# Block attention by pairs of heads in the second block of a two-block transformer kernel

## What is computed

```python
s_own = jnp.einsum('bhqd,bhkd->bhqk', q_c, k_own).astype(f32) + bias_own.astype(f32)[None]
s_own = jnp.where(own_pos[None, :] <= q_pos[:, None], s_own, -jnp.inf)
...
probs = jax.nn.softmax(logits, axis=-1).astype(v.dtype)
...
out = ... + jnp.einsum('bhqk,bhkd->bhqd', p_own, v_own)
```

## Time and profile before

| | us |
|---|---|
| median of 3 runs | 2380.49 (2379.0 to 2385.83) |
| the profiled execution | 2381.41 |
| its span in the profile | 2379.6 |
| TensorE busy in the span | 2307.9 (97%) |
| VectorE busy | 1080.0 (45%) |
| ScalarE busy | 432.1 (18%) |
| mean granted TensorE clock | 0.987 of full speed |

### The profile page before, as it was taken

The page is one execution under the profiler, slowest core; times in us unless marked ns, Lnnn a source line. Parts: engine busy times, 40 slices in busy tenths (PEclk is TensorE's granted clock), DMA queues, the critical chain, the costliest instruction groups (busy, mean ns, idle before and its releaser), DMA issues. The chain is left out here.

```text
span 2379.6 us, 28978 instructions
## 1 busy us (share of the span) xinstructions
PE 2307.9 (97%) x12084; PEld 1560.1 (66%) x12084; DVE 1080.0 (45%) x2030; ACT 432.1 (18%) x850; POOL 47.1 (2%) x76
## 2 busy tenths in 40 slices
PE   6999999999999989999999999999999999999998
PEld 4778854444444468658767768748857867676873
DVE  2788331111111166652453356666663155235674
ACT  1122221111111121100322211101101122221110
POOL 1000000000000010000000000000000000000000
PEclk9999999999999989999999999999999999999999
DMA  9656569999999954444230444436544242134541
GB/s 397 242 225 270 197 202 371 422 422 422 422 422 422 401 164 158 165 162 151 76 135 20 159 151 158 161 124 212 177 159 176 93 156 90 43 136 150 177 168 44
DMA packets 175981, 499.74 MB, mean 210 GB/s; under 512 B 6888, under 2 KB 99320, under 8 KB 146048
## 3 DMA queue, kind: packets, MB, share of 16 engines
q1 hardware_dynamic: 171904, 481.23, 53.7%
q0 software_dynamic: 3824, 16.43, 2.2%
q10 hardware_dynamic: 144, 0.52, 0.1%
HBM read 491.34 MB, written 6.82 MB: 209 GB/s over the span
## 5 line engine op out<-in xcount | busy, mean ns | idle before, releaser
L2104 PE MATMUL bank<-Tw,Sx 128*128 128x256 f32 x960 | 213.8, 379 | 0.0
L2104 PEld LDWEIGHTS bank<-Tw,Sx 128*128 128x128 f32 x960 | 179.3, 190 | 22.7
L2192 PE MATMUL bank<-xT,ring 128*128 128x256 f32 x704 | 152.6, 379 | 0.0
L862 PE MATMUL bank<-xT,ring 128*128 128x256 f32 x640 | 143.4, 384 | 2.8 <-ACT xT L279 2.8
L2192 PEld LDWEIGHTS bank<-xT,ring 128*128 128x128 f32 x704 | 133.4, 190 | 18.0
L2104 PE MATMUL bank<-ring,xT 128*128 128x256 f32 x640 | 144.7, 379 | 0.0
L862 PEld LDWEIGHTS bank<-xT,ring 128*128 128x128 f32 x640 | 122.6, 193 | 21.8 <-ACT xT L279 2.9
L2104 PEld LDWEIGHTS bank<-ring,xT 128*128 128x128 f32 x640 | 121.6, 190 | 18.2 <-issue 1.9
L1425 PE MATMUL bank<-ring,xg 128*64 128x512 f32 x512 | 113.9, 593 | 5.3 <-DMA ring<-in_w 5.3
L1462 PE MATMUL bank<-ring,hTg 128*64 128x512 f32 x512 | 113.4, 595 | 0.0
L1425 PE MATMUL bank<-more,xg 128*64 128x512 f32 x512 | 112.6, 592 | 0.0
(11 more groups left out here) (515 smaller groups left out, 3602.6 us busy)
## 6 DMA issues: line engine op xcount, KB each, us to landing
ring<-in_w SPq DMA_DIRECT2D x128, 1024.0 KB, 17.5
ring<-in_ffn_w_in SPq DMA_DIRECT2D x88, 1024.0 KB, 7.7
ring<-in_first_pieces SPq DMA_DIRECT2D x33, 2048.0 KB, 12.1
more<-in_w SPq DMA_DIRECT2D x64, 1024.0 KB, 17.3
ring<-in_ffn_w_out SPq DMA_DIRECT2D x20, 2048.0 KB, 7.9
ring<-in_w_mix_in SPq DMA_DIRECT2D x12, 2048.0 KB, 7.7
ring<-in_xattn_w_kv SPq DMA_DIRECT2D x8, 2048.0 KB, 8.0
ring<-in_w_mix_out SPq DMA_DIRECT2D x4, 2048.0 KB, 9.8
```

Of the source, the lines that this page charges most:

```text
L862: last = nc.tensor.matmul(b[:, c * SEQ:(c + 1) * SEQ], w[:, k, m * P:(m + 1) * P], xT[:, k, :], start=(k == 0), stop=(k == KD - 1))
L2104: last = nc.tensor.matmul(bank[BANK_OF[name]][:, 0:SEQ], lhs(k), rhs(k), start=(k == 0), stop=(k == 3))
L2192: last = nc.tensor.matmul(b[:, c * SEQ:(c + 1) * SEQ], w[:, k, col:col + P], xT[:, k, :], start=(k == 0), stop=(k == KD - 1))
```

## The change

The loop over eight heads becomes one over four pairs on all three engines. TensorE now issues the scores of both heads product by product in turns (low rows, high rows), the transposes of both heads in a row, and the values of both heads in turns (low columns, high columns). A filler is cut in two parts per pair, one ahead of the values and one behind. `mats(l, 1)` and `mats(l, 3)` stand with one row half at the end of the pairs 0 and 1 and with the other behind the scores in the pairs 1 and 2. ScalarE does the two copies of a pair, then the two exponentials of the next pair; the exponential of head 1 comes ahead of `take_kv(3)`. VectorE does the two `probs` of a pair, then the two `logits` of the next, then the `diagonal` and `inverse_start` calls. No tile, bank or DMA is added, and the count of products is the same.

```diff
--- before.py
+++ after.py
@@ -2309,36 +2309,45 @@
                             last.then_inc(mat_full, 1)
 
             def moba_attention(l):
-                def scores(h):
-                    r = slice((h % 2) * 64, (h % 2) * 64 + 64)
-                    if h >= 2:
-                        pe.wait_ge(mb_sb, l * NH + (h - 1))
-                    b = bank[4 + h % 2]
-                    nc.tensor.matmul(b[:, 0:P], qm[r, h // 2, 0:P], km[r, h // 2, 0:P], start=True, stop=True)
-                    nc.tensor.matmul(b[:, P:384], qm[r, h // 2, P:SEQ], km[r, h // 2, :],
-                                     start=True, stop=True).then_inc(at_s, 1)
-
-                def turned(h):
-                    pe.wait_ge(at_p, l * N_AT + (h + 1))
-                    if h >= 2:
-                        pe.wait_ge(at_tc, l * N_AT + (h - 1))
-                    b = bank[6 + h % 2]
-                    for c, (dst, src) in enumerate(((0, 0), (P, P), (2 * P, 2 * P))):
-                        last = nc.tensor.transpose(b[:, dst:dst + P], sm[:, h % 2, src:src + P], eye)
-                    last.then_inc(at_t, 1)
-
-                def values(h):
-                    pe.wait_ge(at_tc, l * N_AT + (h + 1))
-                    r = slice((h % 2) * 64, (h % 2) * 64 + 64)
-                    o = bank[2 + h // 4][r, ((h // 2) % 2) * SEQ:((h // 2) % 2 + 1) * SEQ]
-                    hs = slice(h * 64, (h + 1) * 64)
-                    nc.tensor.matmul(o, vm[:, 0, hs], pmT[:, h % 2, 0:SEQ], start=True, stop=False)
-                    nc.tensor.matmul(o[:, P:SEQ], vm[:, 1, hs], pmT[:, h % 2, SEQ:384],
-                                     start=False, stop=True).then_inc(at_o, 1)
+
+
+                def half(h):
+                    return slice((h % 2) * HD, (h % 2) * HD + HD)
+
+                def scores(p):
+                    if p:
+                        pe.wait_ge(mb_sb, l * NH + 2 * p)
+                    heads = (2 * p, 2 * p + 1)
+                    for h in heads:
+                        nc.tensor.matmul(bank[4 + h % 2][:, 0:P], qm[half(h), p, 0:P], km[half(h), p, 0:P],
+                                         start=True, stop=True)
+                    for h in heads:
+                        nc.tensor.matmul(bank[4 + h % 2][:, P:384], qm[half(h), p, P:SEQ], km[half(h), p, :],
+                                         start=True, stop=True).then_inc(at_s, 1)
+
+                def turned(p):
+                    pe.wait_ge(at_p, l * N_AT + (2 * p + 2))
+                    if p:
+                        pe.wait_ge(at_tc, l * N_AT + 2 * p)
+                    for h in (2 * p, 2 * p + 1):
+                        for c in range(3):
+                            last = nc.tensor.transpose(bank[6 + h % 2][:, c * P:(c + 1) * P],
+                                                       sm[:, h % 2, c * P:(c + 1) * P], eye)
+                        last.then_inc(at_t, 1)
+
+                def values(p):
+                    pe.wait_ge(at_tc, l * N_AT + (2 * p + 2))
+                    heads = (2 * p, 2 * p + 1)
+                    o = bank[2 + p // 2][:, (p % 2) * SEQ:(p % 2 + 1) * SEQ]
+                    for h in heads:
+                        nc.tensor.matmul(o[half(h), :], vm[:, 0, h * HD:(h + 1) * HD], pmT[:, h % 2, 0:SEQ],
+                                         start=True, stop=False)
+                    for h in heads:
+                        nc.tensor.matmul(o[half(h), P:SEQ], vm[:, 1, h * HD:(h + 1) * HD], pmT[:, h % 2, SEQ:384],
+                                         start=False, stop=True).then_inc(at_o, 1)
 
                 pe.wait_ge(lora_act, (l + 1) * N_LORA)
                 scores(0)
-                scores(1)
                 cross_kv(l, 1)
                 bonus(l)
                 cross_kv(l, 2)
@@ -2347,26 +2356,27 @@
                 mats(l, 2)
                 cross_kv(l, 3)
 
-                low, high = range(0, 4), range(4, KD)
+                quarters = [range(n, n + 2) for n in range(0, KD, 2)]
                 if l == 0:
-                    fill = {0: [(6, low)], 1: [(6, range(4, 6))], 2: [(6, range(6, KD))], 3: [(7, range(0, 2))],
-                            4: [(7, range(2, 4))], 5: [(7, range(4, 6))], 6: [(7, range(6, KD))]}
+                    fill = [((6 + p // 2, quarters[2 * (p % 2)]), (6 + p // 2, quarters[2 * (p % 2) + 1]))
+                            for p in range(NH // 2)]
                 else:
-                    fill = {0: [(4, low), (4, high)], 1: [(5, low)], 2: [(5, high)], 3: [(6, low)], 4: [(6, high)],
-                            5: [(7, low)], 6: [(7, high)]}
-                for h in range(NH):
-                    if h == 0:
+                    fill = [((4 + p, range(0, 4)), (4 + p, range(4, KD))) for p in range(NH // 2)]
+                for p in range(NH // 2):
+                    if p == 0:
                         pe.wait_ge(mat_dve, l * N_MDVE + 4)
-                    turned(h)
-                    if h + 2 < NH:
-                        scores(h + 2)
-                    if h == 4:
+                    turned(p)
+                    if p < NH // 2 - 1:
+                        scores(p + 1)
+                    if 0 < p < 3:
+                        mats(l, 2 * p - 1, (1,))
+                    cross_kv(l, *fill[p][0])
+                    if p == 2:
                         pe.wait_ge(mat_dve, l * N_MDVE + 8)
-                    values(h)
-                    for g, ks in fill.get(h, ()):
-                        cross_kv(l, g, ks)
-                    if h < 4:
-                        mats(l, 1 + 2 * (h // 2), (h % 2,))
+                    values(p)
+                    cross_kv(l, *fill[p][1])
+                    if p < 2:
+                        mats(l, 2 * p + 1, (0,))
 
             def rwkv_heads(l):
 
@@ -2727,20 +2737,25 @@
                 for g in range(3):
                     take_kv(g)
                 expo(0)
+                expo(1)
                 take_kv(3)
-                for h in range(NH):
-                    if h + 1 < NH:
-                        expo(h + 1)
-                    act.wait_ge(at_t, l * N_AT + (h + 1))
-                    if h >= 2:
-                        act.wait_ge(at_o, l * N_AT + (h - 1))
-                    nc.scalar.activation(pmT[:, h % 2, :], bank[6 + h % 2][:, 0:384], ACT.Copy).then_inc(at_tc, 1)
-                    if h % 2 and (l or h > 3):
-                        take_kv(4 + h // 2)
-                    if h % 4 == 3:
-                        act.wait_ge(at_o, l * N_AT + (h + 1))
-                        m = 4 + 2 * (h // 4)
-                        nc.scalar.activation(flat(xT[:, m:m + 2, :]), bank[2 + h // 4][:, :],
+                for p in range(NH // 2):
+                    for h in (2 * p, 2 * p + 1):
+                        act.wait_ge(at_t, l * N_AT + (h + 1))
+                        if p:
+                            act.wait_ge(at_o, l * N_AT + (h - 1))
+                        nc.scalar.activation(pmT[:, h % 2, :], bank[6 + h % 2][:, 0:384], ACT.Copy).then_inc(at_tc, 1)
+                    if p < NH // 2 - 1:
+                        expo(2 * p + 2)
+                        expo(2 * p + 3)
+                    if l:
+                        take_kv(4 + p)
+                    elif p % 2:
+                        take_kv(6 + p // 2)
+                    if p % 2:
+                        act.wait_ge(at_o, l * N_AT + (2 * p + 2))
+                        m = 4 + 2 * (p // 2)
+                        nc.scalar.activation(flat(xT[:, m:m + 2, :]), bank[2 + p // 2][:, :],
                                              ACT.Copy).then_inc(mb_oc, 1)
                 for idx in (6, 7, 4, 5):
                     if idx == 4:
@@ -3161,13 +3176,11 @@
                 dve.wait_ge(bias_loaded, 16)
                 dve.wait_ge(mem_loaded, 64)
                 logits(0)
-                for h in range(NH):
-                    if h + 1 < NH:
-                        if h >= 1:
-                            dve.wait_ge(at_t, l * N_AT + h)
-                        logits(h + 1)
-                    probs(h)
-                    if h == 0:
+                logits(1)
+                for p in range(NH // 2):
+                    probs(2 * p)
+                    probs(2 * p + 1)
+                    if p == 0:
                         for n in range(2):
                             dve.wait_ge(heads_psum, l * N_HEADS + (n + 3))
                             last = nc.vector.tensor_tensor(flat(bon[:, 2 * n:2 * n + 2, :]), bank[6 + n][:, :],
@@ -3178,11 +3191,15 @@
                         for ch in range(2):
                             for e in range(2):
                                 diagonal(2 * ch, e, Lt, C_LOWER)
-                    elif h <= 4:
-                        ch, e = (h - 1) // 2, (h - 1) % 2
-                        diagonal(2 * ch + 1, e, X, C_LEV)
-                        if e == 1:
-                            inverse_start(ch)
+                    if p < NH // 2 - 1:
```

(8 more changed lines are left out.)

## The result

| | us, median | runs | against before, 95% interval |
|---|---|---|---|
| before | 2382.79 (2379.0 to 2386.51) | 15 | |
| changed | 2387.89 (2384.66 to 2393.49) | 15 | 1.0021 (1.0014 to 1.0028) |

The change makes the kernel 0.2% slower, 5.1 us between the medians. The forecast was 2379.5 us, 1.0 us won, with a range of 2373 to 2387. "No change by more than 0.3%" holds; the sign and the range do not. The profiled execution of the changed kernel took 2388.65 us, its span is 2386.9 (2379.6 before), and its mean granted clock is 0.982 (0.987 before).

The account below looks back on a forecast made before the run. TensorE, busy 97% of the span, was taken to bound the kernel. Gains of 17.3 us (12.6 work, 4.7 waits) less 13.1 for added waits and 3.2 for the clock left 1.0 won: 2379.5 us, range 2373 to 2387.

Parts of the forecast that it names:

- TensorE's work: Paired stage of both layers: scores, values, transposes, fillers and `mats` together save 6.3 us per layer, 12.6 us in all.
- The waits that go: Stage loop: six TensorE waits for copies of transposed probabilities (3.8 us) and one for head 5's probabilities (0.9) vanish, 4.7 us.
- The waits that come: Pairs 0 and 1: TensorE idles 2.5 us before the next transposes, twice per layer, for VectorE's `diagonal` and both `probs`; 10.0 us.
- bonus waits: Ahead of the loop: `probs` of head 1 delays VectorE's bonus products, so TensorE waits 0.9 us longer per layer, 1.8 us.
- The clock: TensorE's granted clock falls after two of the four new 2.5 us waits, 1.6 us each, 3.2 us; possible 0 to 6.4.
- rows 9: Earlier trace after the 2.45 us bonus wait: `cross_kv` takes 8.64 us in place of 7.07, 1.6 us more per clock fall.
- Rival C: Slower: each of six waits, four in the loop and two bonus, lowers the clock, 3.2 us each; 2392.3 us, chance 0.05.
- milder form: One clock fall at each of the four loop waits, or one more at each bonus wait: 2383 to 2386 us, chance 0.07.
- A: Faster: VectorE's order costs less than thought; without the four loop waits and their clock falls 2366.3 us, chance 0.07.
- E: Scores or values stay one behind the other because of the semaphore on each head's last product: 2385 to 2390 us, chance 0.02.
- D: The column halves of the value pairs do not run side by side: 5.2 us more, 2384.7 us, chance 0.03.
- B: The clock never falls behind the four new loop waits: 2376.3 us, still within 0.3%, chance 0.14.

Follow-up runs that it names:

- run with both moves: Changed kernel with VectorE's bonus products ahead of both `probs` and the `diagonal` that closes a pair behind both `probs` of the next: 2355.59 us, 0.9881 of before.
- filled waits: Changed kernel with two products of 512 columns put into each of the four 2.4 us waits of TensorE: 2379.49 us, 0.9980 of before.
- run with the `probs` first: Changed kernel with the `diagonal` that closes a pair put behind both `probs` of the next on VectorE: 2369.80 us, 0.9936 of before.

## Why the prediction was wrong

**TensorE's work.** Forecast 12.6 us saved. The loops of the run with both moves, less their 1.35 us of waits in layer 0, against those before, less theirs, give 6.5 + 6.6 = 13.1. The prices of a score pair (0.86), a value pair (0.79 forecast, 0.80 measured) and the transposes hold, and with them the choice of the earlier trace rows over the rule by which a value pair would have cost 1.44 us.

**The waits that go**: 4.7 us forecast, and all are gone.

**The waits that come**: 2.5 us forecast four times, 2.39 measured, in part because the first of the two `probs` took 0.66 us and not 0.74 (1199.54 to 1200.20). The bonus waits were to grow by 0.9 each and grew by 0.87. The two small ones of layer 0 (1.3 us) do not show in the changed kernel, since the slow stretches hide them, and show at full clock (0.2 + 0.56 + 0.58).

**The clock: this term was mis-sized.** I took two falls of 1.6 us, the price in the earlier trace rows. By the timeline there are three behind the four waits. In pair 1 of layer 0 it is 10.4 us from the transposes to the last `mats` product (1201.00 to 1211.43), against 7.2 for the same rows in the run with both moves (1190.78 to 1197.96): 3.2 us, twice the price of rows 9; the same reading gives 3.2 behind the second wait and 3.3 behind the fourth, and nothing behind the third, the first of layer 1. Over both loops the clock costs 39.28 - 28.14 - 4.78 = 6.4 and 49.82 - 41.59 - 4.78 = 3.4 us, together 9.8, and ahead of the loops another 0.9 more than before. That is 10.7 us against 3.2. With it the stage's sum is -13.1 - 4.8 + 9.6 + 1.7 + 10.7 = 4.1 us lost, the 4.2 measured; it has to come out, since the 10.7 is what the other terms leave, and the evidence for it is the three falls read one by one (9.7) and the 8.4 us of the filled waits. The step that failed is "I take two of four, 3.2 us": the number of falls was left to a middle value, their size was taken from the one row at hand, and the lengthened bonus wait was given no clock at all. Rival C, the clock, had the right mechanism and the right size of one fall, and got a chance of 0.05, and 0.07 in its milder form. It asked for a fall at each of six waits, where three in the loop were enough; its "four times in about 25 us per layer" is wrong, the new waits come twice per layer.

**What hid part of the miss, and what added to it.** The terms other than the clock came out 2.3 us better than forecast (0.5 in TensorE's work, 1.8 in the waits), so that the result stayed within 0.3% of no change is in part luck. Against that, the forecast built on the median of 3 runs, 2380.5 us; 15 runs of the kernel before give 2382.8, and these 2.3 us are in the 8.4 between forecast and result.

**The other rivals.** A (the waits do not come) and E (the pairs do not run side by side) are refuted by the timeline, D by the 0.80 us of a value pair, B by the stretches at 0.50.

**What was left out of the sum**: the "issue" gap behind the stage, below. And one thing stood in the earlier trace rows and was not drawn out: the bonus products had no reason to wait for any `probs`. Moving them alone gives 10 us on the kernel before, twice what the change lost.

## What to carry to other kernels

When two units of work are joined, ask of every engine what now stands ahead of the hand-over: here two heads side by side saved 13 us of TensorE's work as foreseen, and one call of 0.9 us that stood ahead of the hand-over on VectorE took more than that back (18 us, by the run that moves it). Price a wait of a saturated TensorE together with the clock behind it: a wait of 2.4 us cost 5.6 us three times in the changed kernel and up to 7.0 in the run with the bonus products moved, and with one or two products put into it (1.3 or 0.5 us idle) the clock stayed up in the executions profiled. Repairs of this kind need not add up: here the two together gained 32 us where they gave 18 and 9 alone, so try them together before one of them is given up.

## What the hardware showed that was not expected

**A fall of the clock has no fixed price.** The wait of 2.45 us cost 1.6 us in both layers before (9.74 and 9.72 us from its end to the first transposes, where the same rows take 8.10 at full clock); waits of 2.39 us cost nothing once and 3.2 us or a little more three times in the changed kernel, and 4.6, 3.2, 4.5 and 3.3 us in the run with the bonus products moved. The same wait of 3.32 us for the bonus products cost nothing in one layer and 2.6 us in the other of one execution. This is the timeline of TensorE in the run with the `probs` first, layer 0:

```profile
1179.81 1.16 PE L2305 MATMUL bank<-aT,kk 64*128 64x128 f32 x16 [3.32 <-DVE bon L3188]
1180.90 7.17 PE L2257 MATMUL bank<-gm,ring 128*128 128x256 f32 x32
```

and layer 1:

```profile
1927.12 2.08 PE L2305 MATMUL bank<-aT,kk 64*128 64x128 f32 x16 [3.32 <-DVE bon L3188]
```

and a stretch of each, 1.00 and 0.50 granted (the first lies behind the wait, the second begins 1.1 us ahead of its end):

```profile
1181.00:1187.00 6.00, 6.00 (x28) 5.30 (x29) 3.60 (x10) 0.00 (x0) 0.00 (x0) 1.00 0.00 0
1926.00:1932.00 6.00, 4.88 (x23) 4.12 (x24) 5.76 (x14) 0.00 (x0) 0.00 (x0) 0.50 0.00 0
```

TensorE's instructions around the wait are the same in both layers. Four of the profiled executions have this wait of 3.32 us, twice each; against the 29.16 us that layer 0 took here from the first scores to the first transposes, the others took 1.6 and 2.6 us more in the changed kernel, 3.0 and 2.7 with two products in the loop's waits, 3.0 and 2.6 with one, where nothing was changed ahead of the loop. So a long fall does not need the paired work of the loop. Why one fall is longer than another was not tried and stays open.

**A gap without a waiter.** Every kernel with pairs shows TensorE idle in the 64-wide products of the recurrent half, put down to "issue": 2.9 us in two places in the changed kernel, 3.0 with both moves, against 1.1 before and 0.9 in the kernel before with the bonus products moved. Over all kernels with pairs it is 2.2 to 3.7 us. The products there are the same in all of them. Waits of TensorE in the run with both moves:

```profile
PE bank L2395 <- issue: 3.0, 2, 1.6
```

So about 1.8 us of the 5.1 lost may be this gap and not the stage. What it comes from was not tried, but the traces give two leads. First, the gap stands at a fixed place of TensorE's stream of instructions, not at a fixed product: in layer 0 it has 38 rows of its group of 64 behind it in the changed kernel, 42 where one product was put into each wait of the loop (4 rows more ahead of the gap) and 46 where two were (8 more); in layer 1 it is 22, 30 and 38. Second, the DMA view has a queue named `instruction`. One packet of it moves in the half microsecond from 1239.84, right ahead of the gap that the changed kernel has from 1240.34 to 1242.06, while the queue of the weights still moves data (56% of the time of the 16 DMA engines from 1236 to 1240.3). In layer 0 of the kernel before, the weights are through earlier (1.7% from 1234 to 1236), and there is no such gap. Both would fit a TensorE that waits for instructions which arrive late behind other transfers; that this is the cause is not shown.
